# Two fused transformer blocks on one core: three edits to the order of work around the tensor engine

## The chip, the core and the metric

The kernel runs on one core of a Trainium2 chip. Its engines run side by side, each with its own instruction stream: TensorE (PE; PEld is its weight load), VectorE (DVE), ScalarE (ACT), GpSimd (POOL) and SyncE (SP), which here only issues DMAs. They wait for each other on counting semaphores that the program names. The time is the device time of one execution of the whole program, in microseconds. A profile is one such execution, taken by the hardware profiler.

## The reference

Two blocks of two layers each, on 1024 tokens of width 1024, all in float32. The first block's layer, shortened:

```python
h = rms_norm(x, g_pre)
q_h, f_h, i_h, z_h, q_a, k_a, v_a, z_a = split(h @ w_in)       # w_in: 1024 x 6400
o_h = rms_norm(hgrn2(q_h, f_h, i_h, lb), g_head) * silu(z_h)   # 8 recurrent heads of 128
q_a, k_a = rotary(q_a), rotary(k_a)                            # 16 query heads of 64, 2 key heads
o_a = sliding_window_attention(q_a, k_a, v_a, sinks) * silu(z_a)
y = concat(o_h, o_a) @ w_out                                   # 2048 -> 1024
x = x + rms_norm(y, g_post)
```

The second block puts 16 meta tokens in front (1040 tokens) and in each layer computes

```python
f_in, q, k, v, gate = split(rms_norm(x, norm_gain) @ w_in)     # 1024 -> 3072
f_out = real(fft2(f_in per group of 128 channels)) @ w_f       # 4 groups, over tokens and channels
a_out = rms_norm(diff_attention(q, k, v, lam)) * (1 - lambda_init)
x = x + (concat(f_out, a_out) * silu(gate)) @ w_out
```

## The kernel before

Every float32 product is made of three matmuls: the weights' high part by the data's high and low part, and the weights' low part by the data's high part. The data of a layer's input stand in `H`, high (`H[:, 0]`) and low (`H[:, 1]`), by eight tiles of 128 channels. Of the weights, `raw` has two slots of 128 columns each (512 KB, loaded by SP), and POOL makes `whi` and `wlo` from them in `split_in`: a CAST and a subtraction. Such a split waits until TensorE is done with the tile that stood in its slot.

Three places of this program are changed.

**Pairs of the sliding-window attention** (first block, both layers). The 16 query heads are worked on in 8 pairs, each in 8 steps of 128 queries, 64 steps in all. In a step TensorE does the scores (L1130), a piece of a projection, the values of two steps back (L1152), another piece, and the transposes of the step before (L1140). The pieces belong to four projection items per pair, of two steps each: in the list `pair_items`, L142, pair p computes the gates z of its own heads and the queries q of the next pair, in halves of 512 tokens. Queries have weight slot 0, gates slot 1; `pair_tile` (L150) gives a tile's number in the order in which POOL splits them. A finished item is copied out of its PSUM bank by ACT two steps after it began. For queries, SP then issues four DMAs of 64 KB that rotate the rows (`RQ<-QR`), and POOL makes the rotary product in three operations (`roped`, L779 on: L786, L787, L788). DVE does the softmax of each step: L2218 (mask), L2221, L2224, L2227, L2230, L2234 (the probabilities' scaling, two operations, for which L1140 waits), L2238, L2239.

**The end of a first block's layer.** The second half of `y` is made for eight blocks s of 128 tokens, each in 16 steps t of three matmuls (L1208). DVE and ACT finish block s-1 meanwhile: DVE normalises it and adds the residual (`finish`), ACT squares the sum (`new_rows`, L1483), DVE scales it (`scale_out`) into the next layer's input. During the last block, s = 7, TensorE also turns the first half of the next input (L977, `turn`), eight tiles of 4 transposes: four ahead of t = 0, four more between the later steps. Such a later one needs the PSUM bank of the tile four before it, so it waits in `fresh` until ACT (`high_in`, L1479) and DVE (`low_in`, L2000) have written that tile into `H`. `high_in` itself waits for `hw_free`, since `H` still holds the weights of the steps 2u and 2u+1.

**The Fourier mixer of the second block.** Its token transform multiplies by two tables of cosines and sines, high and low. ACT casts the second table (`table_high`, L1748), DVE makes its low part (`table_low`, L2307) after folding the first group (`fold`, L2318 and L2319). TensorE computes `along_width` (L1252, 20 matmuls, which read the folded group `UF` and `AW`), a tile of projections (L1236, 72 matmuls) and then `along_tokens` (L1261), which reads the tables and the parts `UH` and `UL` that ACT (L1777) and DVE (L2328) make from the result of `along_width`.

Of the kernel before, what the change touches and what calls it, by code (L numbers as in the profile page):

```python
# [19 lines left out]
DT = D // P  # L20
S = 1024
ST = S // P
# [13 lines left out]
PAIRS = 8  # L36
# [97 lines left out]
WP_A = W_A // 2  # L134
# [6 lines left out]
def pair_items(p):  # L141

    if p < 0:
        return [("q", 0, 0), ("q", 0, 1)]
    if p < PAIRS - 1:
        return [("q", p + 1, 0), ("z", p, 0), ("q", p + 1, 1), ("z", p, 1)]
    return [("z", p, 0), ("z", p, 1)]


def pair_tile(kind, p):  # L150

    if kind == "q":
        return 2 * p + 2 if p < 2 else 2 * p + 1
    return 3 if p == 0 else min(2 * p + 4, 2 * PAIRS + 1)


EXP_TANH = "exp_and_others"
# [104 lines left out]
def build(nc, x, w_in, w_out, g_pre, g_post, lb_param, g_head, sinks, meta, norm_gain2, w_in2, w_fourier, q_gain2, k_gain2,  # L262
          lambda_q1, lambda_k1, lambda_q2, lambda_k2, subln_gain, w_out2, consts, lvl_mask, rope_tab, lam_tab, rope2_tab, dft, out):
    ctx = ExitStack()
    with ctx:
# [387 lines left out]
        def _(pool):  # L653
# [46 lines left out]
            with pool.Fori(0, DEPTH) as L:  # L700
# [91 lines left out]
                roped(0, 1)  # L792
                for p in range(PAIRS - 1):
                    roped(p + 1, 0)
                    if p < PAIRS - 2:
                        split_in(L * WP_A + e0 // 2 + 3 + p, 0, i0 + PAIR_ITEM[("q", p + 1, 1)] + 1)
                    roped(p + 1, 1)
                    split_in(L * WP_A + e0 // 2 + 2 + p, 1, i0 + PAIR_ITEM[("z", p, 1)] + 1)


                end_phase(pool, phase, "ph_pool")
# [166 lines left out]
        def _(pe):  # L968
# [29 lines left out]
            with pe.Fori(0, DEPTH) as L:  # L998
# [191 lines left out]
                for s in range(ST):  # L1190
                    pe.wait_ge(g("y0_ready"), L * ST + s + 1)
                    if s == 6:
                        turn_meta(L, 2, XMA)
                    if s == 7:
                        pe.wait_ge(g("xn_ready"), (L + 1) * ST + 6)
                        for u in range(4):
                            turn(L + 1, u, 2 + u)
                    for t in range(CT):
                        th = t // 8
                        if s == 7 and t in (4, 6, 8, 10):  # L1200
                            fresh(L + 1, t // 2 - 2)
                            turn(L + 1, t // 2 + 2, t // 2)
                        if t % 8 == 0:
                            pe.wait_ge(g("cl_ready"), L * 2 * CT + CT + 2 * s + th + 1)
                        if s == 0:
                            pe.wait_ge(g("w_split"), L * W_A + e0 + CT + t + 3)
                        for n, (c, part) in enumerate(((CHI, 0), (CHI, 1), (CLO, 0))):
                            last = nc.tensor.matmul(bank(s), c[:, th, t % 8, :], H[:, part, t * 512:t * 512 + 512],  # L1208
                                                    start=t == 0 and n == 0, stop=t == CT - 1 and n == 2)
                        if t == 7 and s < 7:  # L1210
                            last.then_inc(g("ch_used"), 1)
                        elif s == 7 and t % 2 and t < CT - 1:
                            last.then_inc(g("hw_free"), 1)
                    last.then_inc(g("y_ready"), 1)
# [4 lines left out]
            with pe.Fori(0, DEPTH) as L:  # L1219
# [34 lines left out]

                def along_tokens(gr):
                    pe.wait_ge(g("ul_ready"), (L * GROUPS + gr) * 3 + 3)
                    for m in range(2):
                        for f, (a, n) in enumerate(FCH):
                            for j in range(JT):
                                for k, (u, t) in enumerate(((UH, TH), (UH, TL), (UL, TH))):  # L1260
                                    last = nc.tensor.matmul(psum[4 + 2 * m + f][:, 0:n], u[:, j, m, :], t[:, m, j * NFP + a:j * NFP + a + n],  # L1261
                                                            start=j == 0 and k == 0, stop=j == JT - 1 and k == 2)
                    last.then_inc(g("pq_ready"), 1)
# [15 lines left out]
                project2(1, 1, 4, 1, cols=CHF)  # L1279
                project2(1, 1, 5, 2, cols=CHF)  # L1280
                pe.wait_ge(g("awc_ready"), L + 1)
                pe.wait_ge(g("tabl_ready"), L * 2 + 2)
                for gr in range(GROUPS):
                    along_width(gr)
                    if gr < GROUPS - 1:
# [167 lines left out]
        def _(act):  # L1453
# [54 lines left out]
            with act.Fori(0, DEPTH) as L:  # L1508
# [183 lines left out]
                    square_out(L, s, XT2[:, s % 2, :])  # L1692

                for s in range(ST):
                    if s:
                        new_rows(s - 1)
                    if s == 4:
# [3 lines left out]
                    if s < ST - 1:  # L1701
                        high(CT + 2 * s + 2)
                        high(CT + 2 * s + 3)
                    else:
                        for u in range(DT - 1):
                            act.wait_ge(g("hw_free"), L * (DT - 1) + u + 1)
                            high_in(L + 1, u, 2 + u % 4)
                    act.wait_ge(g("y_ready"), L * 2 * ST + ST + s + 1)
# [266 lines left out]
        def _(dve):  # L1975
# [82 lines left out]
            with dve.Fori(0, DEPTH) as L:  # L2058
# [207 lines left out]
                for s in range(ST):  # L2266
                    if s == 5:
                        scale_meta(L, XMA, XMA)
                    if s == 6:
                        gain_meta(L, 2, MTA)  # L2270
                    if s:
                        scale_out(L, s - 1, XT2[:, (s - 1) % 2, :])
                    if s < ST - 1:
                        low(CT + 2 * s + 2)
                        low(CT + 2 * s + 3)
                    else:
                        for u in range(DT - 1):
                            low_in(L + 1, u, 2 + u % 4)
                        dve.wait_ge(g("y_ready"), L * 2 * ST + 2 * ST)
                        place_meta(MTA)  # L2280
# [248 lines left out]
```

## Time and profile before

| | us |
|---|---|
| median of 3 runs | 3689.04 |
| lowest, highest | 3680.05, 3689.48 |
| the profiled execution | 3686.93 |
| its span (first to last instruction) | 3685.1 |
| PE busy | 3400.6 |
| DVE busy | 2055.3 |
| ACT busy | 1570.5 |
| POOL busy | 1462.5 |

The span is what the trace covers; 1.8 us of the execution lie outside it. The mean granted TensorE clock is 0.967 of full speed: in some stretches the trace shows the lower of two levels (1.2 instead of 2.4 GHz), and there each matmul takes longer.

### The profile page before, as it was taken

To read this page: it belongs to the slowest core of one execution; us is meant where nothing else is said; L and a number is where in the kernel's file an instruction comes from. 1 tells how busy PE (TensorE), PEld (TensorE's weight loads), DVE (VectorE), ACT (ScalarE), POOL (GpSimd) and SP (SyncE) were. 2 spreads that over 40 slices of the span, in tenths; PEclk is the share of its full clock that TensorE was granted. 3 is DMA by queue.
4 is the path that set the end of the run, shared out by engine and by line. 5 is a ranking of instruction groups with operands and counts; after the bars stand their busy time and mean duration, and the time that the engine had idled before them with its cause. 6 is when DMAs were issued, how large, how long until landed. Compare 5 with 4: busy or idle time off the path is not lost.

```text
span 3685.1 us, 59943 instructions
## 1 busy us (share of the span) xinstructions
PE 3400.6 (92%) x18080; PEld 2758.4 (75%) x18080; DVE 2055.3 (56%) x5230; ACT 1570.5 (43%) x3221; POOL 1462.5 (40%) x1830
## 2 busy tenths in 40 slices
PE   8999999998999999999998989889888999889878
PEld 6888886665878888876666779777775798777756
DVE  5666665665256666656664351366553322665543
ACT  6444443443245444533443341354553322555532
POOL 6555544333516555553335311233242122323341
PEclk9999999998999999999999999999998999999989
DMA  4111112111221111121112231110121512111124
GB/s 146 35 35 33 31 39 62 38 41 44 83 93 38 35 35 29 34 63 35 44 32 73 78 97 47 55 38 27 43 77 44 158 50 63 34 37 38 39 72 146
DMA packets 217950, 206.47 MB, mean 56 GB/s; under 512 B 17948, under 2 KB 185260, under 8 KB 216668
## 3 DMA queue, kind: packets, MB, share of 16 engines
q1 hardware_dynamic: 197536, 137.80, 13.4%
q0 software_dynamic: 12208, 47.03, 3.7%
q10 hardware_dynamic: 7920, 18.19, 1.6%
q8 instruction: 136, 2.23, 0.3%
q14 instruction: 150, 1.23, 0.1%
HBM read 148.04 MB, written 37.01 MB: 50 GB/s over the span
## 4 chain that ended last, share of the span: by engine, by line
PE 70%; DVE 10%; issue 9%; ACT 5%; DMA 2%; POOL 1%; DVEq 1%; SPq 1%; ACTq 0%; POOLq 0%
PE banks L1015 23%; PE banks L1299 7%; PE banks L1184 5%; PE banks L1236 5%; PE banks L1317 4%; PE banks L1208 4%; PE banks L1381 4%; PE banks L1130 2%; PE banks L1372 2%; PE banks L1261 2%; PE banks L1140 2%; PE banks L1152 1%; PE banks L1053 1%; DVE BB L2082 1%; PE banks L1359 1%
## 5 line engine op out<-in xcount | busy, mean ns | idle before, releaser
L1015 PE MATMUL banks<-H,whi 128*128 128x512 f32 x3200 | 1048.8, 409 | 20.1 <-POOL wlo L672 18.3
L1015 PEld LDWEIGHTS banks<-H,whi 128*128 128x128 f32 x3200 | 574.8, 189 | 199.1 <-issue 80.1
L1015 PE MATMUL banks<-H,wlo 128*128 128x512 f32 x1600 | 633.4, 396 | 0.0
L669 POOL CAST whi<-raw 128x1024 fp32r<-128x1024 f32 x150 | 165.5, 1103 | 1030.8 <-PE banks L1015 428.2
L672 POOL TENSOR_TENSOR wlo<-raw,whi 128x256 fp32r<-128x256 f32 (+1 forms) x246 | 406.0, 1666 | 12.1
L1299 PE MATMUL banks<-H,whi 128*128 128x346 f32 (+1 forms) x1536 | 386.6, 335 | 9.9 <-DVEq L423 8.0
L2393 DVE TENSOR_SCALAR_CACHE_REDUCE SP<-banks 128x346 f32<-128x346 f32 (+3 forms) x432 | 202.1, 512 | 280.1 <-PE banks L1360 278.2
L1015 PEld LDWEIGHTS banks<-H,wlo 128*128 128x128 f32 x1600 | 302.5, 189 | 69.5
L1299 PEld LDWEIGHTS banks<-H,whi 128*128 128x128 f32 x1536 | 276.6, 196 | 17.4 <-issue 14.0
L1661 ACT ACTIVATE SM<-SM,stt 128x256 f32<-128x256 f32 (+1 forms) x256 | 124.8, 488 | 332.6 <-DVE stt L2239 332.6
L1299 PE MATMUL banks<-H,wlo 128*128 128x346 f32 (+1 forms) x768 | 253.2, 330 | 0.0
L2105 DVE TENSOR_TENSOR EX<-EX,QB 128x128 f32<-128x128 f32 (+1 forms) x448 | 241.5, 563 | 2.3 <-issue 0.3
L2218 DVE TENSOR_TENSOR SM<-banks,cst 128x512 f32<-128x512 f32 (+1 forms) x128 | 84.2, 658 | 201.2 <-PE banks L1130 201.2
L1359 PE MATMUL banks<-KM,QH 128*128 128x346 f32 (+3 forms) x432 | 161.6, 376 | 29.5 <-DMA QH<-QH 19.3
L1236 PE MATMUL banks<-H,whi 128*128 128x346 f32 (+3 forms) x768 | 184.2, 325 | 3.3 <-DVE H L2035 2.1
L1372 PE MATMUL banks<-cst,SP 128*128 128x128 f32 (+3 forms) x648 | 99.3, 291 | 80.2 <-DVE SP L2403 50.5
L1184 PE MATMUL banks<-H,CHI 128*128 128x512 f32 x512 | 165.3, 404 | 8.4 <-DVE CLO L2250 8.4
L1927 ACT ACTIVATE SP<-SP,st 128x1040 f32<-128x1040 f32 x144 | 166.3, 1158 | 15.0 <-DVE st L2458 14.6
L1208 PE MATMUL banks<-H,CHI 128*128 128x512 f32 x512 | 164.4, 402 | 1.5 <-DVE CLO L2250 1.5
L2115 DVE COPY AT<-banks 32x32 f32<-32x32 f32 (+1 forms) x384 | 76.4, 199 | 147.2 <-PE banks L1060 122.7
L672 POOL TENSOR_TENSOR H<-raw,H 128x256 fp32r<-128x256 f32 (+2 forms) x128 | 149.9, 1185 | 19.7 <-POOL H L669 18.1
L2105 DVE TENSOR_TENSOR EX<-EX,KB 128x128 f32<-128x128 f32 (+1 forms) x448 | 153.3, 368 | 2.0
(311 smaller groups left out, 7386.6 us busy)
## 6 DMA issues: line engine op xcount, KB each, us to landing
raw<-in_w_in SPq DMA_DIRECT2D x148, 512.0 KB, 4.0
raw<-in_w_out SPq DMA_DIRECT2D x64, 256.0 KB, 2.6
XT<-x_resident POOLq DMA_DIRECT2D x18, 512.0 KB, 4.1
x_resident<-XT POOLq DMA_DIRECT2D x18, 512.0 KB, 2.9
raw<-in_w_out SPq DMA_DIRECT2D x18, 512.0 KB, 4.9
RQ<-QR SPq DMA_DIRECT2D x112, 64.0 KB, 2.0
XB<-x_resident POOLq DMA_DIRECT2D x14, 512.0 KB, 4.8
SR<-cat_resident SPq DMA_DIRECT2D x16, 448.0 KB, 4.2
```

The lines of the kernel that those rows point to most:

```text
L669: link(nc.gpsimd.tensor_copy(hi, src))
L672: last = nc.gpsimd.tensor_tensor(lo[:, a:a + n], src[:, a:a + n], hi[:, a:a + n].bitcast(F32), ALU.subtract)
L1015: last = nc.tensor.matmul(bank(half if bk is None else bk), w[:, slot, k, :], H[:, part, a:a + 512], start=k == 0 and n == 0, stop=k == DT ...
L1184: last = nc.tensor.matmul(bank(s), c[:, t % 2, s, :], H[:, part, t * 512:t * 512 + 512], start=t == 0 and n == 0, stop=t == CT - 1 and n == 2)
L1208: last = nc.tensor.matmul(bank(s), c[:, th, t % 8, :], H[:, part, t * 512:t * 512 + 512], start=t == 0 and n == 0, stop=t == CT - 1 and n ...
L1236: last = nc.tensor.matmul(psum[item % 2][:, 0:n], w[:, slot, k, :], H[:, part, k * T2 + a:k * T2 + a + n], start=k == 0 and m == 0, stop=k ...
L1299: last = nc.tensor.matmul(bk[:, 0:n], w[:, slot, k, :], H[:, part, k * T2 + a:k * T2 + a + n], start=k == 0 and m == 0, stop=k == DT - 1 a ...
L1359: nc.tensor.matmul(bk, QH[:, c, q0:q0 + nq], KM[:, h % 2, c, a:a + n], start=True, stop=False)
L1372: last = nc.tensor.transpose(psum[5 + (3 * t + n) % 2][0:m, at * P:at * P + nq], SP[0:nq, t % 2, 0, a:a + m], ident[0:nq, 0:nq])
L1927: last = nc.scalar.activation(SP[0:nq, t % 2, c, :], SP[0:nq, t % 2, c, :], ACT.Exp, scale=-1.0, bias=st[:, 8 + c:9 + c], accum_out=st[:, ...
L2105: return V.tensor_tensor(e, e, x, ALU.mult)
L2393: V.tensor_scalar(SP[0:nq, t % 2, c, a:a + n], psum[2 + k % 3][0:nq, 0:n], -1.0, None, ALU.mult, ALU.min, accum_out=st2[0:nq, t % 2, 3 * c ...
```

## The change

It has three parts. In `pair_items` the gates' items come ahead of the next queries' (z, q, z, q in place of q, z, q, z), the tiles are numbered to match, and POOL splits the next gate tile ahead of the second query tile and ahead of the rotary product of the second half. At s = 7, ACT and DVE write the first two tiles of the next input ahead of what they do for block 6, and TensorE's four later turns stand at t = 8, 10, 12, 14 in place of 4, 6, 8, 10. The wait for the tables' low parts stands in `along_tokens` of the first group, no longer ahead of the first `along_width`.

```diff
     if p < PAIRS - 1:
-        return [("q", p + 1, 0), ("z", p, 0), ("q", p + 1, 1), ("z", p, 1)]
+        return [("z", p, 0), ("q", p + 1, 0), ("z", p, 1), ("q", p + 1, 1)]
     return [("z", p, 0), ("z", p, 1)]
 def pair_tile(kind, p):
-    if kind == "q":
-        return 2 * p + 2 if p < 2 else 2 * p + 1
-    return 3 if p == 0 else min(2 * p + 4, 2 * PAIRS + 1)
+    return 2 * p + (2 if kind == "q" else 3)
...
                 for p in range(PAIRS - 1):
                     roped(p + 1, 0)
+                    split_in(L * WP_A + e0 // 2 + 2 + p, 1, i0 + PAIR_ITEM[("z", p, 1)] + 1)
                     if p < PAIRS - 2:
                         split_in(L * WP_A + e0 // 2 + 3 + p, 0, i0 + PAIR_ITEM[("q", p + 1, 1)] + 1)
                     roped(p + 1, 1)
-                    split_in(L * WP_A + e0 // 2 + 2 + p, 1, i0 + PAIR_ITEM[("z", p, 1)] + 1)
...
-                        if s == 7 and t in (4, 6, 8, 10):
-                            fresh(L + 1, t // 2 - 2)
-                            turn(L + 1, t // 2 + 2, t // 2)
+                        if s == 7 and t in (8, 10, 12, 14):
+                            fresh(L + 1, t // 2 - 4)
+                            turn(L + 1, t // 2, t // 2 - 2)
...
                 def along_tokens(gr):
                     pe.wait_ge(g("ul_ready"), (L * GROUPS + gr) * 3 + 3)
+                    if gr == 0:
+                        pe.wait_ge(g("tabl_ready"), L * 2 + 2)
...
                 pe.wait_ge(g("awc_ready"), L + 1)
-                pe.wait_ge(g("tabl_ready"), L * 2 + 2)
...
                 for s in range(ST):
+                    if s == ST - 1:
+                        for u in range(2):
+                            act.wait_ge(g("hw_free"), L * (DT - 1) + u + 1)
+                            high_in(L + 1, u, 2 + u % 4)
                     if s:
                         new_rows(s - 1)
...
-                        for u in range(DT - 1):
+                        for u in range(2, DT - 1):
                             act.wait_ge(g("hw_free"), L * (DT - 1) + u + 1)
                             high_in(L + 1, u, 2 + u % 4)
...
+                    if s == ST - 1:
+                        low_in(L + 1, 0, 2)
+                        low_in(L + 1, 1, 3)
                     if s:
                         scale_out(L, s - 1, XT2[:, (s - 1) % 2, :])
...
-                        for u in range(DT - 1):
+                        for u in range(2, DT - 1):
                             low_in(L + 1, u, 2 + u % 4)
```

No instruction is added or taken away; line numbers shift by a few in the changed program. POOL's stream in one pair of the attention, before:

```order
L786 TENSOR_TENSOR QR<-QR,ropet 128x512 [waits rot_in0]
L787 TENSOR_TENSOR RQ<-RQ,ropet 128x512
L115 ISA
L788 TENSOR_TENSOR QR<-QR,RQ 128x512 [waits pool_chain]
L679 ISA
L667 ISA [waits proj_ready]
L669 CAST whi<-raw 128x1024 [waits w_in0]
L115 ISA
L672 TENSOR_TENSOR wlo<-raw,whi 128x1024 [waits pool_chain]
L782 ISA
L786 TENSOR_TENSOR QR<-QR,ropet 128x512 [waits rot_in1]
```

and POOL's stream at the same place now:

```order
L786 TENSOR_TENSOR QR<-QR,RQ 128x512 [waits pool_chain]
L677 ISA
L665 ISA [waits proj_ready]
L667 CAST whi<-raw 128x1024 [waits w_in1]
L115 ISA
L670 TENSOR_TENSOR wlo<-raw,whi 128x1024 [waits pool_chain]
L677 ISA
L665 ISA [waits proj_ready]
L667 CAST whi<-raw 128x1024 [waits w_in0]
L115 ISA
L670 TENSOR_TENSOR wlo<-raw,whi 128x1024 [waits pool_chain]
L780 ISA
```

`w_in0` is the load of a query tile, `w_in1` that of a gate tile: the gate tile's split has moved up between the first half's rotary product and the query tile's split. ACT's stream at the start of block s = 7, before:

```order
L1711 ACTIVATE ssy<-ssy,eps 128x1 [waits act_chain]
L1691 ISA
L1483 ACTIVATE XN,rstat<-XT 128x8x128 [waits xo_ready]
L115 ISA
L1485 ACTIVATE rstat<-rstat,eps 128x1 [waits act_chain]
L1700 ACTIVATE sqy,ssy<-Y 128x512
L115 ISA
L1706 ISA [waits act_chain]
```

and now:

```order
L1714 ACTIVATE ssy<-ssy,eps 128x1 [waits act_chain]
L1696 ISA
L1476 ISA [waits hw_free]
L1478 ACTIVATE H<-banks,gpre 128x512 [waits tr_ready]
L1696 ISA
L1476 ISA [waits hw_free]
L1478 ACTIVATE H<-banks,gpre 128x512 [waits tr_ready]
L1690 ISA
L1482 ACTIVATE XN,rstat<-XT 128x8x128 [waits xo_ready]
```

Two of the writes into `H` now stand between block 6's last small operation and the wait for block 6's sum (`xo_ready`). TensorE's stream ahead of the first `along_width`, before:

```order
L1282 ISA [waits awc_ready]
L1246 ISA [waits tabl_ready]
L1252 MATMUL banks<-AW,UF 105x128 [waits fold_ready]
L1252 MATMUL banks<-AW,UF 105x128 x9
L1226 ISA
L1227 ISA [waits w_split]
L1236 MATMUL banks<-H,whi 128x348 [waits proj_free]
```

and now:

```order
L1244 ISA [waits awc_ready]
L1250 MATMUL banks<-AW,UF 105x128 [waits fold_ready]
L1250 MATMUL banks<-AW,UF 105x128 x9
L1224 ISA
L1225 ISA [waits w_split]
L1234 MATMUL banks<-H,whi 128x348 [waits proj_free]
```

The wait for `tabl_ready` is gone from here; it stands 92 matmuls later, beside the wait for `ul_ready`.

## Rows read from the trace of the kernel before

**Rows 1.** The page, busy time of each engine.
```profile
PE 3400.6 (92%) x18080; PEld 2758.4 (75%) x18080; DVE 2055.3 (56%) x5230; ACT 1570.5 (43%) x3221; POOL 1462.5 (40%) x1830
```
**Rows 2.** Waits of PE: line waited for: us in total, times, longest us.
```profile
PE banks L1015 <- POOL wlo L672: 18.3, 4, 6.7
PE banks L977 <- DVE H L2000: 16.6, 5, 6.2
PE banks L1140 <- DVE SM L2234: 16.4, 35, 1.7
```
**Rows 3.** Timeline, PE, block 7: start us, us, line, tile, count [idle before].
```profile
1077.35 0.71 PE L1208 MATMUL banks<-H,CHI 128*128 128x512 f32 x2
...
1085.26 1.11 PE L977 MATMUL banks<-cst,XN 128*128 128x128 f32 x4 [4.87 <-DVE H L2000]
...
1091.10 0.60 PE L977 MATMUL banks<-cst,XN 128*128 128x128 f32 x4
...
1094.13 0.63 PE L1208 MATMUL banks<-H,CHI 128*128 128x512 f32 x2
...
1097.64 0.63 PE L1015 MATMUL banks<-H,whi 128*128 128x512 f32 x2
...
2164.05 1.12 PE L977 MATMUL banks<-cst,XN 128*128 128x128 f32 x4 [4.86 <-DVE H L2000]
```
**Rows 4.** Timeline, DVE, the same block of the first layer.
```profile
1080.71 0.68 DVE L2262 TENSOR_TENSOR XT<-banks,XT 128x512 f32<-128x512 f32 x1
...
1084.45 1.41 DVE L2000 SCALAR_TENSOR_TENSOR H<-banks,gpre,H 128x512 fp32r<-128x512 f32 x2 [0.57 <-ACT H L1479]
```
**Rows 5.** Timeline, ACT, the same block, and the start of the pairs.
```profile
1081.43 1.06 ACT L1483 ACTIVATE XN<-XT 128x1024 f32<-128x1024 f32 x1 [3.26 <-DVE XT L2262]
...
576.40 1.07 ACT L1519 ACTIVATE VT<-banks 128x512 f32<-128x512 f32 x2
```
**Rows 6.** Timeline, PE, the Fourier mixer's first groups in both layers.
```profile
2213.70 4.59 PE L1252 MATMUL banks<-AW,UF 128*105 128x128 f32 x20 [6.61 <-DVE TL L2307]
2217.94 0.93 PE L1236 MATMUL banks<-H,whi 128*128 128x348 f32 x2
...
2219.74 0.49 PE L1236 MATMUL banks<-H,whi 128*128 128x348 f32 x2
...
2230.24 0.29 PE L1261 MATMUL banks<-TH,UH 105*128 105x262 f32 x1
...
2249.02 2.35 PE L1252 MATMUL banks<-AW,UF 128*105 128x128 f32 x20
...
2967.68 3.82 PE L1252 MATMUL banks<-AW,UF 128*105 128x128 f32 x20 [6.61 <-DVE TL L2307]
```
**Rows 7.** Timeline, DVE, the Fourier mixer's first group.
```profile
2205.57 0.15 DVE L2320 COPY UF<-UT 128x2 f32<-128x2 f32 x1
2209.80 3.77 DVE L2307 TENSOR_TENSOR TL<-ST,TH 105x2610 fp32r<-105x2610 f32 x1 [4.08 <-ACT TH L1748]
2218.95 1.62 DVE L2328 TENSOR_TENSOR UL<-banks,UH 105x512 fp32r<-105x512 f32 x3 [5.38 <-ACT UH L1777]
```
**Rows 8.** Timeline, PE, the first layer's pairs: their start, and pair 7.
```profile
581.80 1.21 PE L1015 MATMUL banks<-H,whi 128*128 128x512 f32 x2 [6.69 <-POOL wlo L672]
...
586.06 0.49 PE L1130 MATMUL banks<-KD,QR 64*128 64x128 f32 x4
...
861.95 1.22 PE L1015 MATMUL banks<-H,whi 128*128 128x512 f32 x2 [2.56 <-POOL wlo L672]
```
**Rows 9.** Timeline, POOL, the start of the first layer's pairs.
```profile
584.21 1.28 POOL L788 TENSOR_TENSOR QR<-QR,RQ 128x512 f32<-128x512 f32 x1
597.86 1.27 POOL L786 TENSOR_TENSOR QR<-QR,ropet 128x512 f32<-128x512 f32 x1 [12.37 <-DMA RQ<-QR]
```
**Rows 10.** Timeline, DVE, steps 2 and 3 of pair 0: the probabilities' scaling.
```profile
593.25 0.62 DVE L2234 TENSOR_SCALAR SM<-SM,stt 128x256 f32<-128x256 f32 x2
...
597.86 2.71 DVE L2234 TENSOR_SCALAR SM<-SM,stt 128x256 f32<-128x256 f32 x2
```

## The prediction

> **What bounds the kernel now.** The first view is the busy time of each engine: TensorE is at work for 3400.6 of the 3685.1 us of the span, no other engine for more than 56% [rows 1]. So time is won only where TensorE waits, or where it runs at the lower of its two clock levels, which in this trace follows a wait of some microseconds. The second view is the list of TensorE's waits [rows 2]: the reader is to see that three groups of it belong to the three edits. The first matmul of a pair item waits for POOL's split of weights, 18.3 us in 4 waits; the turns of the next input wait for DVE, 16.6 us in 5, two of which are the 4.87 and 4.86 us in block 7 [rows 3]; the first `along_width` waits for the low table, 6.61 us in each layer [rows 6]. The timelines around these places then give what ends each wait and what comes next.
>
> **Block 7.** TensorE turns tile 4 at 1085.26, after 4.87 us of waiting, and the whole stretch from t = 0 to the next layer's first matmul lasts 1097.64 - 1077.35 = 20.3 us [rows 3]. Undisturbed it would be shorter: a step takes 0.70 us (five steps from 1094.13 to 1097.64), a turn 0.46 us (from 1091.10 to 1094.13 stand two turns and three steps), so 16 x 0.70 + 4 x 0.46 = 13.1 us. The difference, 7.2 us, is the wait and the half clock behind it. Is the new order undisturbed? ACT is idle for 3.26 us until 1081.43 [rows 5], so from 1078.2. It can write tile 0 once step 1 is through (1078.8) and tile 1 once step 3 is (1080.2), by 1080.9. DVE ends block 6's sum at 1080.71 + 0.68 = 1081.4 and then needs 1.41 us for two low tiles [rows 4], so until 1082.8. The turn at t = 8 falls at 1077.35 + 5.6 = 1083.0 and needs the first of the two, the one at t = 10 needs the second 1.9 us later. ACT's square of block 6 still starts at 1081.43, since it waits for the sum; so tiles 2 and 3 are written where 0 and 1 are now, until 1084.45 + 1.41 = 1085.9, ahead of the turns at 1086.8 and 1088.6. The margins are 0.8 us or more. No DMA and no POOL work is moved here. What follows is `finish` of block 7, which starts from the last step as it does now. Both layers: 2 x 7.2 = 14.4 us. Bounds: nothing if a new wait of the same length takes its place, 15 if the turns hide completely.
>
> **Table wait.** `along_width` needs the folded group, ready at 2205.57 + 0.15 [rows 7], and could start when TensorE is free, at 2213.70 - 6.61 = 2207.1. Removed are 6.61 us in each layer, and the half clock behind them: 4.59 instead of 2.35 us for the 20 matmuls, and 1.80 instead of 0.95 us for the two first projection steps (a step is 0.477: 22 of them from 2219.74 to 2230.24), 3.1 us in layer 0; 3.82 - 2.35 = 1.5 in layer 1 [rows 6]. What is late next: `along_tokens` would start at 2207.1 + 2.35 + 24 x 0.477 = 2220.9. The low table ends at 2209.80 + 3.77 = 2213.6 and the parts `UL` need 1.62 us more [rows 7], 2215.2 at best: 5.7 us of cover. ACT, which casts `UH` between, is through with its table cast when DVE starts at 2209.80. Sum: 13.2 + 3.1 + 1.5 = 17.8 us; bounds 13 and 18.
>
> **Pairs, the start.** Now the first piece is a query tile whose split stands behind a rotary product on POOL; TensorE waits 6.69 us for it and then takes 4.26 us to the first scores [rows 8] where four steps of 0.70 are 2.8. The gate tile was split before. What ends the wait then is the PSUM bank, which ACT empties with the first of two copies at 576.40 (1.07 us for both) [rows 5]: 577.0, so 4.8 us earlier. But POOL's work stays where it is, with the second rotary product ending at 584.21 + 1.28 = 585.5 [rows 9]; now the first softmax steps lie beside it. That costs, by what follows.
>
> DVE's scaling of the probabilities takes 0.62 us, and 2.71 us where POOL's rotary operations of 1.27 us start at the same moment (597.86 on both) [rows 9, 10]: each of its two operations waits for a whole POOL operation. The Trainium skill, page SBUF — State Buffer, section Who interferes with whom, says that VectorE and GpSimd share a port pair that whoever issues first holds for the whole instruction while the other fully blocks. This row agrees; by the rule the new places of POOL's work, not its amount, decide, which is what speaks against this part of the change.
>
> So of 4.8 us and 1.5 us of half clock I take back two POOL operations (2.5 us) and 0.8 us of clock, since the 1.9 us still waited may bring the lower level: 3 us in each layer, 6 in all. Bounds: 0 and 12.6.
>
> **Pairs, the middle.** The rotary products move by two steps, the gate tile's split comes a little later in the pair and directly behind a rotary product, the query tile's split goes to the pair's end. TensorE's waits for the scaling are 16.4 us in 35 waits [rows 2], each the mark of such a collision. Their number can't fall to zero, since nothing is taken away; the gate split, which now starts in the tail of a rotary product, shares one step's collision with it. I take 5 us as won, a third of the row; bounds 16 won and 16 lost. Slack: the second half's queries are needed by the fifth step of the next pair and their rotary product ends in about the third; the gate tile is split a step ahead of its use. SP issues the same DMAs in the same order.
>
> **Pair 7.** Its gate tile's split is late now: 2.56 us of waiting [rows 8], and about 1.5 us of half clock as above, 8 us in both layers. That goes, since the tile is split in pair 6. In its place the second half's rotary product moves into pair 7, where a step has two projection steps less and the softmax is the tightest: one collision of two POOL operations, 2.5 us, and half a microsecond of clock. Won: 8 - 6 = 2 us, bounds 8 and -4.
>
> **Sum.** 14.4 + 17.8 + 6 + 5 + 2 = 45.2 us, from the profiled execution's 3686.93: 3641.7. The median of the three runs is 3689.04, 2.1 us above; half of that goes on top: 3643.
>
> **Rivals.** *The pairs give nothing*: collisions eat what start and pair 7 give. For it: the port is busy as long as before, and the waits in rows 2 are set by tenths of a microsecond of phase. Against it: the two waits for splits do go. Time: 3686.9 - 14.4 - 17.8 = 3654.7, with the same shift 3656.
>
> *One of the two other waits comes back in place*: ACT's or DVE's tile is late for t = 8 (margin 0.8 us), or `UL` for `along_tokens`. Against it: the margins above. Time: some 8 us less is won, 3651.
>
> *Slower*: the port. There are 28 half rotations in pairs 0 to 6 of both layers. If each falls on the scaling as the one at 597.86 does, TensorE waits up to 1.7 us for it (the longest) [rows 2], and the lower clock follows such waits for another 1.5 us: 3.2 us each, 90 us, against 16.4 now. From (32.2 + 16.4) / 28 = 1.7 us per rotation on the kernel is slower than before; with 2.5 us each it takes 3686.9 - 32.2 - 16.4 + 70 = 3708. Against it: most of today's 35 waits are below half a microsecond (16.4 / 35), at several different phases.
>
> **Numbers.** The forecast 0.69, its own range 3633 to 3652; pairs give nothing 0.17; a wait comes back 0.08; slower 0.03; and 0.03 for several of these together with a result near the time before. About 0.3%, 11 us, is what a measurement of this kernel can tell from no change. Faster 0.94, within 0.03, slower 0.03. The range 3628 to 3660 takes in the first two rivals and a pair stage that wins 15 us more than I take.
>
> **What would show it.** Right: in block 7 no turn waits more than a few tenths and the stretch is 13 us; the first `along_width` follows the projections within 0.3 us and takes 2.35 us, with no wait at the first `along_tokens`; the wait for POOL's splits falls from 18.3 to near 0 (the start waits for ACT's copy, about 2 us); TensorE's waits for L2234 (a few lines on) are near 16 us with a new large one in pair 7. Wrong: a wait of 4 us at t = 8 to 14; a wait for `UL`; waits for the scaling above 40 us in sum.

## The result, and the profile after

The changed kernel takes 3636.8 us (median of four runs, 3632.92 to 3641.37) against 3689.26 for the one before in the same set: a ratio of 0.9866, 95% interval 0.9853 to 0.9879. That is 49 us (45 to 54) where 45.2 were summed up; the median lies 6 us below the 3643 forecast. The profiled execution, which the sum speaks of, went from 3686.93 to 3641.37, 45.6 us less. That these two figures agree to 0.4 us is in part luck, as the account by stages shows.

The page and TensorE's waits (line waited for: us in total, times, longest us) answer to [rows 1, 2]:

```profile
PE 3386.5 (93%) x18080; PEld 2745.7 (75%) x18080; DVE 2055.7 (56%) x5230; ACT 1570.7 (43%) x3221; POOL 1461.6 (40%) x1830
```
```profile
PE banks L1138 <- DVE SM L2237: 21.7, 34, 2.0
...
PE banks L975 <- DVE H L2003: 7.2, 4, 6.2
...
PE banks L1261 <- DVE UL L2334: 4.7, 2, 2.3
...
PE banks L1013 <- ACT VT L1518: 3.9, 2, 1.9
```

L1138 and L2237 are the transposes and the scaling that stood at L1140 and L2234; turn, project and scores are now L975, L1013 and L1128. The wait of the projections for POOL's splits is gone from the list, and 3.9 us for ACT's copy stand there, 1.9 at each start. The turns' wait fell by 9.4 us. Most of the 7.2 us left there is one wait outside the three edits, at the end of the Fourier mixer's layer, where four turns stand as early as those of block 7 did:

```profile
2881.32 1.12 PE L975 MATMUL banks<-cst,XN 128*128 128x128 f32 x4 [6.17 <-DVE H L2003]
```

It was 6.22 us before, and between 0.89 and 6.22 in the fourteen profiles, so totals of the turns' waits, and single executions, differ by it. The wait for the table is gone; `UL`, in a later group, costs 4.7 us, as it does before. The waits for the scaling grew from 16.4 to 21.7; where they grew and where they shrank is told with the stages below.

TensorE in block 7, to be laid beside [rows 3] (start us, us, line, tile, count, idle before):

```profile
1073.76 0.71 PE L1206 MATMUL banks<-H,CHI 128*128 128x512 f32 x2
...
1079.44 0.60 PE L975 MATMUL banks<-cst,XN 128*128 128x128 f32 x4
...
1081.27 0.60 PE L975 MATMUL banks<-cst,XN 128*128 128x128 f32 x4
...
1083.10 0.60 PE L975 MATMUL banks<-cst,XN 128*128 128x128 f32 x4
...
1084.94 0.60 PE L975 MATMUL banks<-cst,XN 128*128 128x128 f32 x4
...
1087.24 0.73 PE L1013 MATMUL banks<-H,whi 128*128 128x512 f32 x2 [0.30 <-issue]
```

No turn waits, and the four stand 1.83 us apart: two steps of 0.70 and a turn of 0.43. The granted clock is 1.00 from the first step to the projection. The Fourier mixer's first group, beside [rows 6]:

```profile
2181.47 2.35 PE L1250 MATMUL banks<-AW,UF 128*105 128x128 f32 x20
2183.58 0.56 PE L1234 MATMUL banks<-H,whi 128*128 128x348 f32 x2
...
2195.11 0.29 PE L1261 MATMUL banks<-TH,UH 105*128 105x262 f32 x1
```

The 20 matmuls follow the projections without a wait and take 2.35 us, not 4.59, and the first product along the tokens waits for nothing: the parts `UL` are ready at 2189.70. The start of the pairs, beside [rows 8], and the one row of pair 7:

```profile
577.10 0.74 PE L1013 MATMUL banks<-H,whi 128*128 128x512 f32 x2 [1.93 <-ACT VT L1518]
...
580.09 0.49 PE L1128 MATMUL banks<-KD,QR 64*128 64x128 f32 x4
...
586.23 0.43 PE L1138 MATMUL banks<-cst,SM 128*128 128x128 f32 x2 [1.43 <-DVE SM L2237]
...
865.16 0.43 PE L1138 MATMUL banks<-cst,SM 128*128 128x128 f32 x2 [1.95 <-DVE SM L2237]
```

The first scores come 6 us earlier (586.06 before), a new wait of 1.43 us gives some of it back in step 1, and pair 7 has one of 1.95 us for the scaling where 2.56 us for a split were.

### The profile page after: what moved, and what is told of

It reads as the page before. It is cut to its first block, busy times and chain, and to the rows that moved or that the text cites. A ratio compares the mean times of both kernels' runs of the same rounds, so it can differ in the third digit from the quotient of the medians.

```text
span 3639.6 us, 59943 instructions
## 1 busy us (share of the span) xinstructions
PE 3386.5 (93%) x18080; PEld 2745.7 (75%) x18080; DVE 2055.7 (56%) x5230; ACT 1570.7 (43%) x3221; POOL 1461.6 (40%) x1830
## 3 DMA queue, kind: packets, MB, share of 16 engines
q1 hardware_dynamic: 197536, 137.80, 13.5%
## 4 chain that ended last, share of the span: by engine, by line
PE 72%; DVE 11%; issue 8%; ACT 6%; DMA 1%; DVEq 1%; ACTq 1%; POOL 0%; SPq 0%; POOLq 0%
PE banks L1013 24%; PE banks L1298 7%; PE banks L1182 5%; PE banks L1234 5%; PE banks L1316 4%; PE banks L1206 4%; PE banks L1380 4%; PE banks L1128 2%; PE banks L1371 2%; PE banks L1261 2%; PE banks L1138 2%; PE banks L1150 2%; PE banks L1051 2%; DVE BB L2085 1%; DVE SM L2237 1%
## 5 line engine op out<-in xcount | busy, mean ns | idle before, releaser
L1013 PE MATMUL banks<-H,whi 128*128 128x512 f32 x3200 | 1046.5, 408 | 5.6 <-ACT VT L1518 3.9
L1013 PEld LDWEIGHTS banks<-H,whi 128*128 128x128 f32 x3200 | 572.8, 188 | 184.9 <-issue 65.7
L1013 PE MATMUL banks<-H,wlo 128*128 128x512 f32 x1600 | 632.2, 395 | 0.0
L1013 PEld LDWEIGHTS banks<-H,wlo 128*128 128x128 f32 x1600 | 301.8, 189 | 69.3
L1358 PE MATMUL banks<-KM,QH 128*128 128x346 f32 (+3 forms) x432 | 161.4, 376 | 29.7 <-DMA QH<-QH 19.3
```

Of the source, the lines that this page charges most:

```text
L1013: last = nc.tensor.matmul(bank(half if bk is None else bk), w[:, slot, k, :], H[:, part, a:a + 512], start=k == 0 and n == 0, stop=k == DT ...
L1358: nc.tensor.matmul(bk, QH[:, c, q0:q0 + nq], KM[:, h % 2, c, a:a + n], start=True, stop=False)
```

## The experiments

For the stages, one measure is used throughout: the time between two marks on TensorE. *Pairs* is from the values' first transposes (573.09 in layer 0 before) to the first turn of block 7 (1075.68; some 186 us of it, behind pair 7, are other work that no edit touches), *block 7* from there to the next projection, *table* from the mixer's first projection (2177.54) to its first product along the tokens (2230.24). Each kernel gives two values, one for each layer.

**One part alone: the table.**

```diff
                 def along_tokens(gr):
                     pe.wait_ge(g("ul_ready"), (L * GROUPS + gr) * 3 + 3)
+                    if gr == 0:
+                        pe.wait_ge(g("tabl_ready"), L * 2 + 2)
...
-                pe.wait_ge(g("tabl_ready"), L * 2 + 2)
                 for gr in range(GROUPS):
                     along_width(gr)
```

> The kernel before with one edit: the wait for the table stands ahead of the first product along the tokens instead of ahead of the first product along the width. Theory of the prediction: the table's wait cost 4.59 + 2.35 us in layer 0 and its like in layer 1, with the half clock behind it, 17.8 us in two layers; 3689.3 - 17.8 = 3671.5 us, the first product along the width starts right behind the projections, and no wait for the table is left at the first product along the tokens. Rival: the wait moves with the edit (the table's transfer is late for the tokens' product too), gain under 4 us, 3685 us or more, with a wait for the table at the first product along the tokens.

(The waits were 6.61 us in each layer, not 4.59 and 2.35, which are lengths of the 20 matmuls; the 17.8 stands.) Measured: 3662.16 us, ratio 0.9942 (0.9926 to 0.9958), so 21 us won (15 to 27). The first product along the width, to be laid beside [rows 6], follows without a wait:

```profile
2206.61 2.35 PE L1252 MATMUL banks<-AW,UF 128*105 128x128 f32 x20
```

The stage takes 43.0 and 43.6 us against 52.7 and 51.9 before. The rival, a wait that only moves, falls.

**One part alone: block 7.** TensorE's turns and both engines' writes:

```diff
-                        if s == 7 and t in (4, 6, 8, 10):
+                        if s == 7 and t in (8, 10, 12, 14):
...
+                    if s == ST - 1:
+                        for u in range(2):
+                            act.wait_ge(g("hw_free"), L * (DT - 1) + u + 1)
+                            high_in(L + 1, u, 2 + u % 4)
...
+                    if s == ST - 1:
+                        low_in(L + 1, 0, 2)
+                        low_in(L + 1, 1, 3)
```

> The kernel before with the edits of the seventh row block only: TensorE's four turns four scores later, and the first two tiles of the next input written by ScalarE and VectorE ahead of the block's rows. Theory of the prediction: 14.4 us in two layers, 3674.9 us; the turns' waits for H (16.6 us in 4) fall to about 7 us, which belong to turns elsewhere, and TensorE stays at full clock from the first step of the block to the next layer's first matmul. Rival: the early writes delay the rows that the block's softmax needs, a wait of about 2 us on VectorE's rows comes in at the first scores and the gain is 6 to 9 us, 3680 to 3683 us.

(What this and the next expectations call scores are the steps t of block 7; there is no softmax in it.) Measured: 3669.62 us, ratio 0.9957 (0.9942 to 0.9971), 16 us won. Block 7 takes 15.14 and 15.78 us, as in the kernel with all edits (15.14 and 15.79), against 21.96 and 23.06. The turns' waits in the whole kernel fall to 4.9 us, none of it in this stretch, and the rival's wait of 2 us isn't there.

**One part alone: the pairs.** The order of the items, the tiles' numbers and the split's place on POOL:

```diff
-        return [("q", p + 1, 0), ("z", p, 0), ("q", p + 1, 1), ("z", p, 1)]
+        return [("z", p, 0), ("q", p + 1, 0), ("z", p, 1), ("q", p + 1, 1)]
...
+                    split_in(L * WP_A + e0 // 2 + 2 + p, 1, i0 + PAIR_ITEM[("z", p, 1)] + 1)
                     if p < PAIRS - 2:
                         split_in(L * WP_A + e0 // 2 + 3 + p, 0, i0 + PAIR_ITEM[("q", p + 1, 1)] + 1)
                     roped(p + 1, 1)
-                    split_in(L * WP_A + e0 // 2 + 2 + p, 1, i0 + PAIR_ITEM[("z", p, 1)] + 1)
```

> The kernel before with the order of the pairs alone: the gate tile of a pair ahead of the next pair's queries. Prediction: 13 us, 3676.3 us. By the trace of the kernel with all edits: 10.4 us, 3678.9 us, of which 2.9 in layer 0 and 7.5 in layer 1, with the waits of the transposes for the scaled scores at about 21.7 us in 34 instead of 16.4 in 35. Rival, that the pairs won only because the other edits changed the phase of their transfers: this kernel would be within 5 us of the one before.

Measured: 3667.39 us, ratio 0.9955 (0.9938 to 0.9973), 17 us won (10 to 23); the waits of the transposes are 21.5 us in 32. The rival falls. But neither 2.9 nor 7.5 came back (by the marks used here the first pair of profiles gives 3.6 and 7.5): the pairs take 497.3 and 497.9 us, 5.3 and 6.7 less than in `before`'s own profile. In the five profiles which leave the pairs' code as it was, that same stretch runs from 502.4 to 509.3 us. So the difference of two single profiles can't price this stage.

**Only the turns moved.**

```diff
-                        if s == 7 and t in (4, 6, 8, 10):
-                            fresh(L + 1, t // 2 - 2)
-                            turn(L + 1, t // 2 + 2, t // 2)
+                        if s == 7 and t in (8, 10, 12, 14):
+                            fresh(L + 1, t // 2 - 4)
+                            turn(L + 1, t // 2, t // 2 - 2)
```

> The kernel before with TensorE's four turns of the seventh block moved four scores later and nothing else: the tiles' writes stay behind the block's rows. Theory one, the late writes set the end: the first low tile is written at about 1085.2 us of the trace before, the turns now ask for it at about 1083, so a wait near 2 us stays in each layer and the gain is 9 to 12 us of the 14.4. Theory two, the turns' place alone decides: no wait above 0.5 us at the turns and the whole 14.4 us, 3674.9 us. Theory three, both edits are needed: a wait of 4 us stays, the clock falls as before and the gain is under 4 us.

Measured: 3679.19 us, ratio 0.9989 (0.9974 to 1.0003): by time alone unclear. The stage tells it: 18.93 and 19.66 us, 6.4 less than before in the two layers. The wait is theory one's, the gain is not, since after the 2.08 us the clock falls, as a row of 1.05 us in place of 0.63 shows:

```profile
1088.02 0.66 PE L977 MATMUL banks<-cst,XN 128*128 128x128 f32 x4 [2.08 <-DVE H L2000]
...
1089.20 1.05 PE L1208 MATMUL banks<-H,CHI 128*128 128x512 f32 x2
```

**Only the writes moved.** The two other pieces of that diff, with the turns left at t = 4 to 10. VectorE's piece:

```diff
+                    if s == ST - 1:
+                        low_in(L + 1, 0, 2)
+                        low_in(L + 1, 1, 3)
                     if s:
                         scale_out(L, s - 1, XT2[:, (s - 1) % 2, :])
```

> The kernel before with ScalarE's and VectorE's writes of the first two tiles moved ahead of the seventh block's rows and nothing else: TensorE's turns stay at the scores 4 to 10. Theory one: the writes wait for the row before to be given free, TensorE asks for the first turn about 1.5 us ahead of them, so a wait of about 2 us a layer stays, and the gain is 9 to 13 us. Theory two, the time of the writes alone decides: no wait, 14 us. Theory three: a wait of 4 us as before, the gain is under 4 us.

Measured: 3671.0 us, ratio 0.9969 (0.9955 to 0.9983), 11 us won. Block 7 takes 16.68 and 17.87 us, 10.5 less than before in the two layers. Here the wait is 1.72 us and the clock stays:

```profile
1083.16 0.66 PE L977 MATMUL banks<-cst,XN 128*128 128x128 f32 x4 [1.72 <-DVE H L2004]
...
1084.36 0.63 PE L1208 MATMUL banks<-H,CHI 128*128 128x512 f32 x2
```

Neither half hides the turns: one leaves 1.7 us of waiting, the other 2.1 and half a clock. Together they leave nothing.

**Rotary products in halves.** From here on the base is the changed kernel. The prediction's rival *slower* rests on the port that VectorE and GpSimd share, so GpSimd's operations are made smaller with no work taken away:

```diff
-                    nc.gpsimd.tensor_tensor(QR[:, p % 2, t], QR[:, p % 2, t] if p else QRAW[:, t], ropet[:, 0, t], ALU.mult)
...
+                    parts = [slice(a, a + 256) for a in range(512 * half, 512 * half + 512, 256)]
+                    for t in parts:
+                        nc.gpsimd.tensor_tensor(QR[:, p % 2, t], QR[:, p % 2, t] if p else QRAW[:, t], ropet[:, 0, t], ALU.mult)
```

> The changed kernel with each of GpSimd's three rotary products of a half split in two of 256 columns. Theory, that a VectorE scaling which starts while GpSimd has one of these operations under way waits for its end (2.7 us instead of 0.62): the longest such wait is halved, the transposes' waits for the scaled scores fall from 21.7 us to 10 or less, and the time by about 10 us, to 3627 us. Rival, that the two engines share the port evenly and only the sum of their work counts: the waits stay near 20 us and the time within 3 us of the changed kernel's 3636.8. Against both: six more starts on GpSimd a half, with its own late end, would show as waits of the products with queries.

(It is three more operations a half, not six.) Measured: 3622.54 us, ratio to the kernel before 0.9836 (0.9822 to 0.9849), 11 us below what the changed kernel's 0.9866 gives. A difference of two such ratios, here and below, is good to 7 to 9 us; the stage bears this one out, since the pairs take 491.3 and 490.6 us against 495.9 to 499.0 in the six values of the undivided new code. The waits for the scaling are 14.8 us in 21, not 10 or less: the steps beside the weights' subtractions keep theirs. The step in which the third rotary product meets the scaling, VectorE and GpSimd of the changed kernel (start us, us, engine, line):

```profile
643.47 1.64 DVE L2237 TENSOR_SCALAR SM<-SM,stt 128x256 f32<-128x256 f32 x2
```
```profile
643.61 1.35 POOL L786 TENSOR_TENSOR QR<-QR,RQ 128x512 f32<-128x512 f32 x1
```

and of the one with halves:

```profile
644.70 1.08 DVE L2243 TENSOR_SCALAR SM<-SM,stt 128x256 f32<-128x256 f32 x2
```
```profile
644.84 1.53 POOL L791 TENSOR_TENSOR QR<-QR,RQ 128x256 f32<-128x256 f32 x2
```

GpSimd works longer (1.53 against 1.35 us) and VectorE is free sooner (1.08 against 1.64): it is the length of one operation that it waits for, not the sum.

**Subtractions in quarters.**

```diff
-                    split_in(L * WP_A + e0 // 2 + 2 + p, 1, i0 + PAIR_ITEM[("z", p, 1)] + 1)
+                    split_in(L * WP_A + e0 // 2 + 2 + p, 1, i0 + PAIR_ITEM[("z", p, 1)] + 1, 4)
                     if p < PAIRS - 2:
-                        split_in(L * WP_A + e0 // 2 + 3 + p, 0, i0 + PAIR_ITEM[("q", p + 1, 1)] + 1)
+                        split_in(L * WP_A + e0 // 2 + 3 + p, 0, i0 + PAIR_ITEM[("q", p + 1, 1)] + 1, 4)
```

> The changed kernel with GpSimd's subtraction for the low part of the pair stage's weights in four parts instead of two. By the theory that a scaling waits for the end of the operation under way, the part of the scaling's waits that falls under these subtractions is halved, the steady steps fall from 5.0 to 5.35 us toward 4.86, and 3 to 6 us are won of the changed kernel's 3636.8. Rival: the subtractions do not hold VectorE up at all, the time stays within 2 us and the transposes' waits near 21.7 us.

(The subtraction is one operation of 1024 columns in the changed kernel, not two as the expectation says.) Measured: 3629.78 us, ratio 0.986 (0.9845 to 0.9876), no difference from 0.9866 that the times can tell. The pairs take 492.1 and 494.8 us, less than in any profile of the undivided code, but the waits are 20.6 us in 32. So the stage speaks for a gain of some 4 us a layer, and by the time it is unclear.

**Both.**

> Both: the rotary products in halves and the subtractions in quarters. If each waits for its own operation's end the gains add up, 12 to 16 us under the changed kernel's 3636.8, about 3623 us, and the transposes' waits for the scaled scores are under 7 us. If the port is shared evenly nothing is won over the rotary halves alone.

Measured: 3615.83 us, ratio 0.9818 (0.9804 to 0.9833); the waits are 9.3 us in 9, the pairs 486.0 and 487.2 us. 18 us are won over the changed kernel by the ratios, 7 more than by the halves alone, which the ratios can't tell from nothing; the stage tells it, 4 us a layer shorter than with the halves alone. The waits miss the 7 us that were expected.

**The changed kernel again**, unedited, as the base of the last set.

> The changed kernel once more, with nothing edited, as the base for the three others of this set and to see how far one stage moves between two profiles of the same code. Theory, that the stretch from the first scores of the first pair to the seventh block's turns wanders by some microseconds with the landing of the rotations: it takes 489 to 495 us in each layer (492.0 and 490.2 in the first profile), while the stages of the table and of the seventh block come back within 0.3 us. Rival, that the 2.9 and 7.5 us which the two layers seemed to win are two fixed amounts of the code: 492.0 and 490.2 come back. Time 3630 to 3642 us by either.

Measured: 3633.38 us, ratio 0.9861 (0.9841 to 0.9881). Block 7 is 15.14 and 15.79, the table 43.0 and 43.6, as before to a few hundredths. From the first scores to block 7 it is 487.4 and 491.4 us where the first profile has 492.0 and 490.2, so this stretch does wander, below the range I gave as well. The time ahead of the first scores differs too, in layer 0, where the same code had 577.10, 0.74 and then full clock above:

```profile
577.00 1.01 PE L1013 MATMUL banks<-H,whi 128*128 128x512 f32 x2 [1.93 <-ACT VT L1518]
...
578.24 1.05 PE L1013 MATMUL banks<-H,whi 128*128 128x512 f32 x2
...
581.53 0.49 PE L1128 MATMUL banks<-KD,QR 64*128 64x128 f32 x4
```

**Rotary products of 16 columns.** In pairs 1 to 7 most of the rotation is left out of the queries.

```diff
-                    t = slice(512 * half, 512 * half + 512)
+                    t = slice(512 * half, 512 * half + (16 if p else 512))
```

> The changed kernel with GpSimd's three rotary products of pairs 1 to 7 cut to 16 of their 512 columns, so the queries of these pairs are left without most of their rotation; waits and instruction counts are the same. Theory, that a VectorE scaling waits for the rotary product under way: the scalings of 1.5 to 1.65 us fall to 0.8 or less, and by the 7.1 us a layer that halves of 256 columns won (scalings at 1.03 to 1.09), 0.35 to 0.45 us more at two scalings a pair gives about 12 us a layer, 3613 us. Rival, that VectorE is late by its own queue in these steps: the scalings stay above 1 us and the gain is under 16 us in all, no more than by the halves.

Measured: 3617.57 us, ratio 0.982 (0.9806 to 0.9835), 15 us below the changed kernel of this set by ratio; by the pairs' stage, 487.4 and 485.9 us, it is 11 a layer. The 15 us lie within the "under 16" of the rival, so the time doesn't decide. The rows do: in the timelines of the two layers no group of mask or scaling is left between 1 and 1.9 us (12 or 13 a layer in the changed kernel), and the waits are 11.9 us in 20. The rival, under which the scalings would stay above 1 us, falls. What is left comes from the other user of the port, and these rows, VectorE and GpSimd, are the cleanest of the study:

```profile
646.04 2.08 DVE L2224 TENSOR_TENSOR stt<-stt 128x2 f32<-128x2 f32 x1
648.04 0.67 DVE L2227 TENSOR_REDUCE stt<-SM 128x2 f32<-128x512 f32 x1
```
```profile
645.72 2.38 POOL L670 TENSOR_TENSOR wlo<-raw,whi 128x1024 fp32r<-128x1024 f32 x1
```

An operation on two columns takes 2.08 us (0.15 or 0.16 elsewhere) and ends at 648.12; the subtraction ends at 648.10.

**Pair 0 whole.** Halves for pairs 1 to 7 only, quarters kept:

```diff
-                    parts = [slice(a, a + 256) for a in range(512 * half, 512 * half + 512, 256)]
+                    step = 256 if p else 512
+                    parts = [slice(a, a + step) for a in range(512 * half, 512 * half + 512, step)]
```

> The kernel with rotary halves and quartered subtractions, but pair 0, whose products stand in the path ahead of the first scores, keeps whole products. Its start was 1.3 to 1.5 us later than the changed kernel's in three of four such stages. Theory: 8.48 us from the values' transposes to the first scores fall back to 6.94 and 2 to 4 us are won over the version with all pairs in halves, 3612 us. Rival, that the later start only shifts the collisions of step 1 with it: no difference beyond 1 us.

Measured: 3616.19 us, ratio 0.9809 (0.9795 to 0.9823). From the transposes to the first scores it is 6.94 in one layer and 8.31 in the other, so a late start comes without halves in pair 0 too, and each goes with the clock: of the 18 starts in the nine profiles with the new pairs, 13 took 6.92 to 6.95 us and 5 took 8.2 to 8.5, those with rows of 1.05 us behind the 1.93 us wait. But 3 of the 5 are among the 4 starts with halves in pair 0 and 2 among the 14 without, so whether the halves make a late start likelier stays open. This kernel and the one with halves everywhere can't be told apart by their times. Its waits:

```profile
PE banks L1145 <- DVE SM L2244: 8.8, 7, 1.7
...
PE banks L1020 <- ACT VT L1525: 3.9, 2, 1.9
```

**Subtractions in two parts.** The same with `, 2)` in place of `, 4)`.

> As the kernel with whole products in pair 0 and halves after it, but the subtractions in two parts of 512 columns instead of four of 256. By the theory that a scaling waits for the end of the operation under way, the longest scaling is 1.6 to 1.9 us instead of 1.65 in the steps with a subtraction, and it comes out 1 to 4 us above the quarters. Rival, that the quarters' own length (2.9 us for the four against 2.43 for the one) costs as much as they free: equal, or faster by up to 2 us.

Measured: 3621.66 us, ratio 0.9826 (0.9811 to 0.984), waits 12.5 us in 11, pairs 488.6 and 490.4 us. It lies 6 us above the quarters, on the side of the theory and beyond its 1 to 4; the two intervals overlap, so the size isn't settled.

The best versions, halves with quarters, reach 0.981 to 0.982 of the kernel before, 16 to 21 us below the changed kernel by its two ratios.

## Why the prediction was right

It was right in the total, and in three of its five terms to within 1 us. The start of the pairs was priced 3.8 us too low and pair 7 1.4 us too high, and these partly cancel. The stages, as means over all profiles that have the old or the new code of a stage, priced for two layers:

| stage | old code | new code | won in two layers | forecast |
|---|---|---|---|---|
| table | 52.5 us (10 values) | 43.3 (6) | 18.4 | 17.8 |
| block 7 | 22.3 (6) | 15.5 (6) | 13.7 | 14.4 |
| pairs, transposes to the third scores | 18.7 (10) | 13.7 (6) | 9.8 | 6 |
| pairs, from there to pair 7 | 270.6 (10) | 268.6 (6) | 4.1 | 5 |
| pair 7, its first seven steps | 29.2 (10) | 28.9 (6) | 0.6 | 2 |

They add up to 46.6 us. The divided kernels aren't counted in it, nor, for block 7, those with half of its edit. The three parts run alone sum to 54 us by their ratios, with intervals of 11 to 13 us each, so nothing speaks against their being independent.

**Table.** Every step held: the wait, the half clock behind it, and the cover at `along_tokens`, where `UL` is ready 5.4 us ahead (2189.70 against 2195.11) and 5.7 were worked out.

**Block 7.** The stretch from t = 0 is 13.5 us, from 1073.76 to 1087.24, against the 13.1 worked out; 0.3 is an issue gap ahead of the projection. The argument was that both edits are needed and that each margin is near a microsecond. The two half edits show it from both sides.

**Start of the pairs.** The mechanism was right and the size too small, 3 us a layer where 4.9 were won. I took back two POOL operations, 2.5 us; the step that collides gives between 0.96 and 2.00 us of waiting in the six starts of the undivided code, 1.5 in the mean. And I charged 0.8 us for the clock behind the 1.9 us wait, in every start. The runs show it in 5 of 18, at some 1.4 us each, 0.4 in the mean.

**Middle.** The mechanism held, and the size nearly, though the sum over the whole kernel hides it: that sum grew, from 16.4 to 21.7 and 21.9 us, where "near 16" was the sign (it is 18.0 to 19.9 us in the four other kernels with the old pairs, so 16.4 was low). Between the third scores and pair 7 the waits for the scaling shrank. The two layers, before and then after:

```profile
PE banks L1140 <- DVE SM L2234: 5.6, 16, 0.7
...
PE banks L1140 <- DVE SM L2234: 7.9, 15, 1.7
...
PE banks L1138 <- DVE SM L2237: 6.7, 14, 1.7
...
PE banks L1138 <- DVE SM L2237: 5.8, 14, 0.9
```

Over all ten old and six new values of this stage the mean falls from 7.8 to 6.1 us, by 1.7 a layer, near the 2.0 by which the stage got shorter, and TensorE has no other wait in it, for splits either. That is a fifth, where I took a third of a row that holds other stages too. Single values of the stage lie up to 6 us apart within one code, so 2.0 is good to about 1 us. What grew are the two new collisions, 1.5 us a start and 1.94 to 2.00 us in each pair 7.

**Pair 7.** The new collision came as foreseen. VectorE's scaling and the second operation of GpSimd's rotary product start together:

```profile
863.47 1.56 DVE L2237 TENSOR_SCALAR SM<-SM,stt 128x128 f32<-128x128 f32 x2
```
```profile
863.48 1.26 POOL L785 TENSOR_TENSOR RQ<-RQ,ropet 128x512 f32<-128x512 f32 x1
```

TensorE waits 1.95 us for it, less than the 2.5 priced. The term that was too small is the clock behind it, half a microsecond: it fell in five of the six new values, which take 27.9 to 29.7 us where the sixth takes 27.5. So nearly all that the split's wait gave back is paid again. The 0.3 us a layer that is left is less than values of one code differ by (27.4 to 30.1 in the old), and can't be told from nothing.

**The rivals.** That the pairs give nothing (0.17) is excluded by the run with the pairs alone. That a wait for a tile of `H` or for `UL` comes back (0.08) is excluded by the rows of block 7 and of the mixer. The rival *slower* needed 1.7 us for each half rotation; the whole price of the rotary products in pairs 1 to 7, by leaving them out, is 11 us a layer for 14 of them by the stage, 0.8 us each, or 0.5 by the time. How much of it was paid before the change too was not tried. The runs bear out a lock of the port. The Trainium skill, page SBUF — State Buffer, section Who interferes with whom, says that a VectorE operation with two inputs from SBUF contends with GpSimd's reads through the shared interface. The row of 2.08 us is such an operation and agrees. The gain from halves is what a lock for the whole instruction predicts and an even sharing does not.

## What to carry to other kernels

Where two engines share a port, look at the length of a single operation on the engine that isn't critical: cutting three products in two cost that engine 0.1 to 0.2 us for each and won 11 us, near a quarter of what the whole change had won. When the waits for a collision are to be compared, compare them by stage: here the sum over the kernel grew while the stage that the term spoke of shrank. When a wait goes, count the lower clock behind it, and when one of about 2 us is left, count it as a chance and not as a price. Compare a stage that depends on when DMAs land over several profiles; here one pair of profiles made a gain of 7.4 us a layer look like 3.6 in one and 7.5 in the other.

## What the runs showed of the hardware

- **The clock after a short wait is not fixed.** Behind the wait of 4.87 us [rows 3] TensorE is at its lower level (1.2 GHz); behind 2.08 us it was in both layers, behind 1.72 us in neither, and behind 1.93 us, the same place and the same code on TensorE, in 5 of 18. Up to the third scores the granted clock is 0.88 or 0.89 in these five and 0.97 or more in the others. In pair 7 it fell at 9 of 10 waits of 2.49 to 2.56 us, at 5 of 8 of 1.94 to 2.00 and at none of 8 of 1.34 to 1.41. The lower level shows as 1.05 us for a pair of matmuls of 0.62.
- **A two-column operation can last 2.08 us.** Small VectorE operations with both inputs in SBUF, 0.15 us as a rule, stood at 0.61 and at 1.22 us beside GpSimd operations of 128x512 elements and at 2.08 beside one of 128x1024; how much they lose hangs on where in the other's operation they begin.
- **Splitting a GpSimd operation is cheap.** The subtraction of 1024 columns takes 2.38 us, four of 256 take 2.8 to 2.9: some 0.16 us for each further operation.
- **Some rotations land late.** Most of these 64 KB transfers land 2.0 us after issue. In layer 0 of the changed kernel, near 800 us, the median of two is 2.9, in a stretch that also holds a packet of an instruction queue; 40 us earlier it is 2.0, with a smaller packet of another such queue:

```profile
q8 instruction: 1, 0.02, 1.1%
...
RQ<-QR SPq DMA_DIRECT2D x2, 64.0 KB, 2.9
```

The rotary product then starts 2.34 us into its step instead of 0.5, and two steps take 5.78 and 6.01 us where 5.37 and 5.01 are usual. The pattern holds in all fourteen profiles. They have 392 such groups of four transfers; in 78 a packet of 16 KB of queue q8 is under way beside them, and in 72 of these some transfer takes over 2.5 us, up to 4.27. In the 314 others none takes more than 2.46. No edit moved these packets, so that they are the cause was not tried, and stays open.
